# One output projection of a two-layer stack, with products of 512 columns in place of two of 256

## The reference, cut to what matters

```
# second layer of the first block: spatial gating mixer, then a SwiGLU feed-forward
u, v = split(gelu(rms_norm(h, mix_norm[1]) @ sg_w_in))     # 1024 -> 2 x 1024
sg   = einsum(tril(w_s), rms_norm(v)) + b_s
h    = h + (u * sg) @ sg_w_out                             # 1024 x 1024: this product is changed
g, p = split(rms_norm(h, ffn2_norm[1]) @ ffn2_w_in[1])     # 1024 -> 2 x 2816: the stage behind it
h    = h + 0.5 * (silu(g) * p) @ ffn2_w_out[1]
```

## Time and profile before

| | |
|---|---|
| Median of 3 runs | 1447.31 us (1446.77 to 1447.53) |
| The profiled execution | 1446.78 us, of which the span from the first to the last instruction is 1445.0 us |
| PE busy | 1429.0 us, 99% of the span |
| PEld busy | 1318.0 us, 91% |
| DVE busy | 1094.9 us, 76% |
| ACT busy | 853.8 us, 59% |
| POOL busy | 272.9 us, 19% |
| Granted TensorE clock, mean | 0.999 of full speed (2.4 GHz) |
| Chain that ended last | PE 79%, DVE 13%, ACT 5% |

### The profile page before, as it was taken

One profiled execution on the slowest core, in us unless ns is written; L12 is line 12 of the kernel. 1 busy time (PEld: TensorE's weight loads), 2 busy tenths in 40 slices (PEclk: granted clock), 3 DMA queues, 4 the chain that ended last, 5 costly groups with the idle time before them and its releaser, 6 DMA issues.

```text
span 1445.0 us, 27301 instructions
## 1 busy us (share of the span) xinstructions
PE 1429.0 (99%) x9633; PEld 1318.0 (91%) x9633; DVE 1094.9 (76%) x2031; ACT 853.8 (59%) x1559; POOL 272.9 (19%) x329
## 2 busy tenths in 40 slices
PE   8999999999999999999999999999999999999998
PEld 7888899988888888889988888999999999999998
DVE  6777679877766777667787766798878779986883
ACT  6665458766544656446566655656757555576762
POOL 1111113121102111014031113332250035121000
PEclk9999999999999999999999999999999999999999
DMA  6667754556655666565456655554344555434533
GB/s 213 197 193 211 234 179 132 183 182 202 183 190 182 190 188 195 183 196 169 155 171 201 186 189 173 163 144 126 92 125 137 171 148 160 126 102 122 148 116 121
DMA packets 247876, 241.25 MB, mean 167 GB/s; under 512 B 15457, under 2 KB 246737, under 8 KB 247785
## 3 DMA queue, kind: packets, MB, share of 16 engines
q1 hardware_dynamic: 244888, 236.73, 53.6%
q10 hardware_dynamic: 2896, 3.30, 0.8%
HBM read 238.92 MB, written 1.07 MB: 166 GB/s over the span
## 4 chain that ended last, share of the span: by engine, by line
PE 79%; DVE 13%; ACT 5%; issue 2%; DMA 1%; ACTq 0%; SPq 0%; DVEq 0%
PE bank L691 72%; DVE w_lo L1866 3%; ACT w_hi L1128 1%; DVE work L2474 1%; DVE work L2423 1%; DVE work L1903 1%; PE bank L1011 1%; DVE y_both L1866 1%; PE bank L995 1%; ACT L1160 1%; DMA raw<-in_ffn_w_in_dram 1%; DVE work L2497 1%; PE bank L978 1%; PE bank L1012 0%; PE bank L994 0%
## 5 line engine op out<-in xcount | busy, mean ns | idle before, releaser
L691 PE MATMUL bank<-x_both,w_hi 128*128 128x512 f32 (+2 forms) x3216 | 747.5, 336 | 1.3 <-DVE w_lo L1866 0.8
L1866 DVE TENSOR_TENSOR w_lo<-raw,w_hi 128x1024 fp32r<-128x1024 f32 (+1 forms) x429 | 519.4, 1234 | 203.2 <-ACT w_hi L1128 202.2
L1128 ACT CAST w_hi<-raw 128x1024 fp32r<-128x1024 f32 (+1 forms) x429 | 429.4, 1028 | 125.2 <-PE bank L691 108.0
L691 PEld LDWEIGHTS bank<-x_both,w_hi 128*128 128x128 f32 x3216 | 467.5, 189 | 4.1 <-DVE w_lo L1866 1.6
L691 PEld LDWEIGHTS bank<-x_both,w_lo 128*128 128x128 f32 x2312 | 405.6, 188 | 62.5
L691 PE MATMUL bank<-x_both,w_lo 128*128 128x256 f32 (+1 forms) x2312 | 461.9, 281 | 0.0
L691 PE MATMUL bank<-y_both,w_hi 128*128 128x512 f32 (+2 forms) x1376 | 331.5, 342 | 1.6 <-DVE w_lo L1866 1.0
L691 PEld LDWEIGHTS bank<-y_both,w_lo 128*128 128x128 f32 x1040 | 184.3, 188 | 31.3
L691 PE MATMUL bank<-y_both,w_lo 128*128 128x256 f32 (+1 forms) x1040 | 206.1, 280 | 0.0
L691 PEld LDWEIGHTS bank<-y_both,w_hi 128*128 128x128 f32 x1376 | 200.2, 189 | 2.5 <-DVE w_lo L1866 1.4
L1753 POOL TENSOR_TENSOR work<-work,rstd 128x256 f32<-128x256 f32 x88 | 66.9, 782 | 412.7 <-ACT work L1197 412.7
(11 more groups left out here) (312 smaller groups left out, 1395.7 us busy)
## 6 DMA issues: line engine op xcount, KB each, us to landing
raw<-in_ffn_w_in_dram SPq DMA_DIRECT2D x176, 512.0 KB, 3.8
raw<-in_w_in_dram SPq DMA_DIRECT2D x100, 512.0 KB, 3.7
raw<-in_ffn_w_out_dram SPq DMA_DIRECT2D x64, 512.0 KB, 4.6
raw<-in_w_out_dram SPq DMA_DIRECT2D x32, 512.0 KB, 4.5
raw<-in_ffn_w_out_dram SPq DMA_DIRECT2D x32, 384.0 KB, 3.4
raw<-in_rec_w_in_dram SPq DMA_DIRECT2D x16, 512.0 KB, 4.3
raw<-in_sg_w_in_dram SPq DMA_DIRECT2D x16, 512.0 KB, 4.3
raw<-in_rec_w_out_dram SPq DMA_DIRECT2D x8, 512.0 KB, 3.5
```

What stands on the lines that cost most here:

```text
L691: i_ = mm(accs[m][:, cols], w[:, j, m * P:(m + 1) * P], moving, start=begin and g == 0 and not residual, stop=final)
L1128: nc.scalar.copy(hi_part(U)[:, 0:n, :], raw[:, s, 0:n, :]).then_inc(hi_made, 1)
L1866: TT(lo_part(U)[:, 0:n, :], raw[:, s, 0:n, :], hi_part(U)[:, 0:n, :].bitcast(fp32), SUB).then_inc(lo_made, 1)
```

## The change

`sg_out` is put into `WIDE_OUT`, and both branches for `EIGHT_TILES` learn what the other output projections do: PE uses the form of 512 columns, and DVE adds first the lower half of the bank to h and then, after a wait for that, the upper half. The residual of `sg_out` is added by DVE before and after. `rec_out`, the other projection with 8 tiles, stays as it is.

```
-WIDE_OUT = ("out01", "out02", "out11", "out12")
+WIDE_OUT = ("out01", "out02", "out11", "out12", "sg_out")

     # PE, out_phase, EIGHT_TILES
-    unit(U, k0, n, pb + p, 0, ys, N, j == 0, j == 1, ready if p == 0 else None, 0)
+    unit(U, k0, n, pb + p, 0, ys, N, j == 0, j == 1, ready if p == 0 else None, 0,
+         both=name in WIDE_OUT)

     # DVE, out_phase, EIGHT_TILES
     for m in range(2) if name not in PE_ADDS else ():
         c = 2 * p + m
         wait_tile(pb + p, m)
+        low = bank[BANK_OF[2 * (pb + p) + m]][:, SEQ:2 * SEQ]
+        link(STT(out=h[:, c, T0:L], in0=low, scalar=half, in1=h[:, c, T0:L], op0=MUL, op1=ADD))
         STT(out=h[:, c, T0:L], in0=tile(pb + p, m, N), scalar=half, in1=h[:, c, T0:L], op0=MUL,
             op1=ADD).then_inc(tile_read, 1)
```

## The result

| | before | after |
|---|---|---|
| Median of 21 runs | 1447.38 us (1446.0 to 1448.97) | 1449.21 us (1447.93 to 1451.36) |
| Profiled execution / span | 1446.78 / 1445.0 us | 1449.08 / 1447.3 us |

The account below looks back on a forecast made before the run. PE is busy 99% of the span, but DVE and ACT set the tail of `sg_out`. Terms 0.53 + 0.16 + 0.08 = 0.77 us later: 1447.55 profiled, 1448.1 on the median; range 1446.5 to 1449.3.

Parts of the forecast that it names:

- PE's products: In `sg_out`, 512 columns save 0.023 us a step: 0.46 by the end of unit 5, 0.74 over 32 steps.
- DVE's evictions, pair by pair: In `sg_out`, first tile 0.46 us later, second 0.91, from pair start; pair 0 hidden, `in12` starts 0.53 late.
- the wait of `in12`: At the start of `in12`, PE waits 1.7 to 1.9 us for tile 4's eviction and starts 0.53 later.
- `norm_sum` (0.16): In `in12`, PE waits 0.16 us because POOL's last sum ends at 732.19 and PE's load stands at 732.10.
- unit 7 (0.08): In `in12`, lower weights ready at 745.25, PE's load at 745.24; with the semaphore, PE waits 0.08 us.
- The 0.07 for the semaphore: At `norm_sum`, 0.07 us added for the semaphore to reach the wait of 0.16.
- the rest of the kernel moves as a whole: After unit 7 of `in12`, DVE gains on PE, its lag of 1.13 us goes within a turn; nothing further added.
- No DMA: Behind the change, no DMA and no semaphore of the weight ring is moved.
- PE's gain: Rival, chance 0.09: added evictions disappear behind ACT in every pair, `in12` starts when PE is ready: 1446.1 to 1446.6 us.
- the whole lag: Rival, chance 0.15: margins at units 5 and 7 are spent, PE late by 1.13 or 1.7: 1448.4 to 1449.0 us.
- The clock rival: Rival, chance 0.04: PE's clock falls in the 1.8 us gap before `in12`, 2.1 lost: 1450.2 to 1451 us.

Follow-up runs that it names:

- e3: Kernel before with only PE's products of 512 columns; DVE adds only each bank's upper half, leaving the lower out of the result: 1447.77 us, ratio 1.0004.
- e7: Kernel after, but the first unit of `in12` makes all four k of its first tile, then those of the second: 1448.21 us, ratio 1.0006 to before.
- e9: Kernel after with `in12`'s first unit done tile by tile and 128 already fulfilled waits added on PE in `sg_out`: 1447.99 us, ratio 1.0007 to before.
- e5: Kernel before with 128 already fulfilled waits added to PE's program in `sg_out`: 1447.59 us, ratio 1.0004.
- e6: Kernel after with 128 already fulfilled waits added to PE's program in `sg_out`: 1449.01 us, ratio 1.0011 to before.
- e10: Kernel before with DVE's split of the next lower weights moved ahead of the inputs' lower parts in `sg_out`: 1446.51 us, ratio 0.9996.
- e2: Kernel before with PE's products of 256 columns kept, but DVE adding each tile in two linked steps of half: 1448.92 us, ratio 1.0011.
- e12: The same kernel as e2 (before with only DVE's two linked additions a tile), profiled again for its clock: 1449.39 us, ratio 1.0014.

## Why the prediction was right and where it failed

- **PE's products**: right. 0.697 a step, 0.72 saved over 31 steps, 0.45 by unit 5 (e3). The row of `out11` was the right one; the estimate from the start-to-start gap, 0.16 for all, would have been far too small.
- **DVE's evictions, pair by pair**: right. Pairs 4.55 apart for 4.6, linked starts 0.45 and unlinked 0.34 apart, `in12`'s first product +0.50 for +0.53, PE idle for 1.69 where some 1.8 was forecast.
- **The first step that failed: the sum took the wait of `in12` as one wait.** The prediction had the second tile coming 0.91 late, 0.46 more than the first, and followed that number to ACT and DVE only. The same lateness releases bank 1, which PE needs 0.23 us after bank 0. It was worth 0.46. In place of 0.53 the start costs 0.96.
- **`norm_sum` (0.16) and unit 7 (0.08)**: sized rightly, but absorbed. POOL's last sum was forecast to end at 732.19 and, with `sg_out` 0.47 later in this execution, ends at 732.62; PE is at `norm_sum` only at 733.11, as it had already stood still for tile 5. With that wait removed they are there: 0.14 and 0.08 in e7, 0.13 and 0.04 in e9. The 0.07 for the semaphore, for which the prediction shows no row, is 0.05 in e7 (732.18 to 732.23). So the missed wait added 0.46 and hid some 0.2 of these two; from the start of `sg_out` to 1038.82's wait it comes to 0.97 in after, 0.72 in e7 and 0.67 in e9, where 0.77 was forecast.
- **The second step that failed: "the rest of the kernel moves as a whole", with "No DMA" moved.** The term was put at nothing; it measures 0.7. The fetches of PE's own instructions are moved, and 430 us behind the change a load on the chain took 0.7 us longer. Controls with the length of PE's program changed and nothing else (e5, e6), and combined with the tile order (e9), move it in the expected direction. Of the 14 profiles, 7 have a fetch within the load, which took 5.03 to 5.34 us; 6 of the 7 others took 4.30 to 4.78. The seventh is e10, with 5.03. In all 14 the stretch from wait to wait follows the load: 222.55 to 223.01 us up to 4.78, 223.26 to 223.59 from 5.03 on. So the load is where the 0.7 arises, and the interventions show that the length of PE's program moves it. That the length acts through the fetch fits 13 of 14 profiles; no run has a changed length without a fetch in the load, and what slowed e10's load stays open.
- **The rivals.** PE's gain did not carry through. Taken as a size, the one of the whole lag was nearest: after's 0.97 lies between my 0.77 and its 1.13, though not by its mechanism, which was stretched splits. The median of 1449.21 lies above that case's 1448.4 to 1449.0 as well. It lies in the range because that ends 0.3 above the case, an allowance for scatter and not a mechanism; that is luck. The clock rival did not occur in after, but it is real: e2 shows it at a gap of 1.41 us, shorter than forecast, with a loss of 1.55 us, less than the 2.1 recorded.
- **What is left.** 0.97 and 0.68 make 1.65 of 1.83 in the medians. In the spans the scatter at the start adds 0.47 and the last stretch 0.18; that stretch takes from 183.10 (e3) to 184.17 us (e2) in the profiles, in no order that I can tie to an edit. Both stay unattributed.

## What to carry to other kernels

Ask which engine sets the end of the stage before making another one faster: 0.45 us gained by PE here stood against 0.96 on DVE, whose evictions set the start of the next stage. When a release gets later, follow it for every buffer that it frees, the second as well as the first. And an edit that changes the number of instructions by a hundred moves the code fetches of the rest of the program, so an effect below 0.1% is judged by stretches of the trace, with a control whose program has the same length.

## What was unexpected on the chip

- A fetch of one packet of 16 KB, 0.8% of the DMA engines' time in 8 us, goes with a load of 512 KB that takes 5.03 to 5.34 us in all seven profiles that have it there, in place of 4.30 to 4.78 in six of the seven others.
- The same kernel, with the same gap of 1.41 us on PE, kept a clock of 1.00 in one profile (e12) and fell to 0.85 and 0.72 in two windows of another (e2).
- 128 instructions on PE that only wait for what is fulfilled already, within 22 us, cost nothing that B shows (31.70 with and without).
